# Gated delta rule: the triangular solve by 32x32 blocks inverted on VectorE, in place of 16x16 blocks joined on TensorE

## The reference, cut to what matters

```
# per head and chunk
Lmat = where(strict, (kb @ k.T) * decay, 0)         # strictly lower triangular
A    = Lmat + eye
rhs  = concat([v * beta, kb * exp(G)])
sol  = triangular_solve(A, rhs, lower, unit_diagonal)   # u, w
v_new = u - w @ S
o     = (q * exp(G)) @ S + attn @ v_new
S     = S * exp(G_last) + k_dec.T @ v_new
```

## Time and profile before

| | |
|---|---|
| median of 3 runs | 2217.33 us (2216.49 to 2218.11) |
| span of the profiled execution | 2215.9 us |
| mean granted TensorE clock | 0.995 |
| TensorE busy | 2178.7 us, 98% of the span |
| VectorE busy | 1499.2 us, 68% |
| ScalarE busy | 1004.1 us, 45% |

### The profile page before, as it was taken

One profiled execution on the slowest core, in us unless ns is written; L12 is line 12 of the kernel. 1 busy time (PEld: TensorE's weight loads), 2 busy tenths in 40 slices (PEclk: granted clock), 3 DMA queues, 4 the chain that ended last, 5 costly groups with the idle time before them and its releaser, 6 DMA issues.

```text
span 2215.9 us, 27209 instructions
## 1 busy us (share of the span) xinstructions
PE 2178.7 (98%) x10552; PEld 1830.3 (83%) x10552; DVE 1499.2 (68%) x1881; ACT 1004.1 (45%) x1286; POOL 25.4 (1%) x26
## 2 busy tenths in 40 slices
PE   6899999999999999999999999999999999999998
PEld 5789988888888888888888888888888888888887
DVE  8988698988888677755455555575546555655556
ACT  5357455433444644443444334465444444444444
POOL 0001000000000000000000000000000000000000
PEclk9999999999999999999999999999999999999999
DMA  9975568977998688866666666666666666666663
GB/s 404 420 275 166 186 220 279 305 244 245 331 337 302 207 277 292 295 219 191 192 191 186 191 197 190 187 203 192 190 197 185 191 194 191 189 192 189 194 190 128
DMA packets 241552, 507.08 MB, mean 229 GB/s; under 512 B 19304, under 2 KB 34960, under 8 KB 235920
## 3 DMA queue, kind: packets, MB, share of 16 engines
q1 hardware_dynamic: 241424, 505.35, 70.2%
HBM read 503.16 MB, written 2.12 MB: 228 GB/s over the span
## 4 chain that ended last, share of the span: by engine, by line
PE 86%; DVE 6%; DMA 4%; ACT 2%; issue 2%; POOL 0%; DVEq 0%; ACTq 0%; POOLq 0%
PE bank L1254 25%; PE bank L1256 25%; PE bank L1255 25%; DVE WL L2080 2%; PE bank L1445 2%; PE bank L1186 2%; PE bank L1261 1%; PE bank L1263 1%; PE bank L1262 1%; DVE RAW L2067 1%; ACT WH L1528 1%; DMA RAW<-in_w_cd_dram 1%; DMA RAW<-in_w_ada_dram 1%; DMA A<-in_w_cq_dram 1%; DMA RAW<-in_w_cq_dram 1%
## 5 line engine op out<-in xcount | busy, mean ns | idle before, releaser
L2080 DVE TENSOR_TENSOR WL<-RAW,WH 128x1024 fp32r<-128x1024 f32 x706 | 859.9, 1222 | 576.7 <-ACT WH L1528 567.3
L1528 ACT CAST WH<-RAW 128x1024 fp32r<-128x1024 f32 x706 | 738.4, 1049 | 849.1 <-PE bank L1256 702.0
L1254 PE MATMUL bank<-WH,HTh 128*128 128x512 f32 x1922 | 758.1, 394 | 1.1 <-DVE WL L2080 1.0
L1256 PE MATMUL bank<-WH,HTl 128*128 128x512 f32 x1922 | 749.1, 390 | 0.0
L1255 PE MATMUL bank<-WL,HTh 128*128 128x512 f32 x1922 | 748.4, 389 | 0.0
L1256 PEld LDWEIGHTS bank<-WH,HTl 128*128 128x128 f32 x1922 | 360.8, 188 | 76.2
L1254 PEld LDWEIGHTS bank<-WH,HTh 128*128 128x128 f32 x1922 | 361.1, 188 | 75.7 <-DVE WL L2080 2.4
L1255 PEld LDWEIGHTS bank<-WL,HTh 128*128 128x128 f32 x1922 | 361.2, 188 | 72.2
L1254 PE MATMUL bank<-WH,R2h 128*128 128x512 f32 x408 | 160.6, 394 | 0.3 <-DVE WL L2080 0.3
L1256 PE MATMUL bank<-WH,R2l 128*128 128x512 f32 x408 | 159.0, 390 | 0.0
L1255 PE MATMUL bank<-WL,R2h 128*128 128x512 f32 x408 | 158.9, 389 | 0.0
(11 more groups left out here) (302 smaller groups left out, 1823.5 us busy)
## 6 DMA issues: line engine op xcount, KB each, us to landing
RAW<-in_a_w_in_dram SPq DMA_DIRECT2D x192, 512.0 KB, 4.2
RAW<-in_w_gate_up_dram SPq DMA_DIRECT2D x176, 512.0 KB, 4.5
RAW<-in_w_ada_dram SPq DMA_DIRECT2D x128, 512.0 KB, 5.5
RAW<-in_w_in_dram SPq DMA_DIRECT2D x112, 512.0 KB, 4.8
RAW<-in_w_down_dram SPq DMA_DIRECT2D x88, 512.0 KB, 4.3
RAW<-in_a_w_out_dram SPq DMA_DIRECT2D x64, 512.0 KB, 4.1
A<-in_w_ada_dram SPq DMA_DIRECT2D x17, 1024.0 KB, 14.0
RAW<-in_w_o_dram SPq DMA_DIRECT2D x32, 512.0 KB, 5.9
```

The costliest lines, as they stand in the source:

```text
L1254: e.matmul(o, ah[:, s], hi[:, k, :], start=first, stop=False)
L1256: i = e.matmul(o, al[:, s], hi[:, k, :], start=False, stop=last)
L1528: e.copy(hi, rv).then_inc(S["hi"], 1)
L2080: e.tensor_tensor(lo, rv, hi.bitcast(F32), ALU.subtract).then_inc(S["lo"], 1)
```

## The change

The diagonal blocks that VectorE inverts are 32x32 now. The column steps run over j = 0 to 30; step j works on (31 - j) rows of min(j + 1, 16) elements per partition, each step again one multiply and one add. They are put in 13 slots (`INV_STEPS`) in place of eight. `X`, `ZT` and `XZ` are gone: a cell spreads one matrix (`XT`) and goes on with `NT`, two slots after it. The layout steps around the inversion change with the block size.

```
-        for j in range(0, 15, 2):
-            self.put("inv", j, j + 2)
+INV_STEPS = [(0, 3), (3, 6)] + [(j, j + 2) for j in range(6, 24, 2)] + [(24, 27), (27, 31)]
+        for j0, j1 in INV_STEPS:
+            self.put("inv", j0, j1)
             yield
...
-        for name in ("X", "ZT", "XZ", "NT") + ("kS",) * tt + ("U", "NU", "NW", "NY", "o"):
+        for name in ("X", "NT") + ("kS",) * tt + ("U", "NU", "NW", "NY", "o"):
...
             for q in range(4):                                   # gdn_pick, ScalarE
                 r = slice(32 * q, 32 * q + 32)
                 e.copy(L.LP[r, :, :, n:n + 4].rearrange("p j b h -> p h b j"),
-                       lm[r, :, r].rearrange("p h (b j) -> p h b j", j=16)).then_inc(S["gdn_pick"], 1)
+                       lm[r, :, r].unsqueeze(2).to_broadcast([32, 4, 2, 32])).then_inc(S["gdn_pick"], 1)
...
+            for b in range(2):                                   # inv_x, ScalarE, 512 elements each
+                e.activation(L.XE[:, :, b, :], L.XB, ACT.Copy, scale=L.bm2[:, b:b + 1]).then_inc(S["gdn_pick"], 1)
...
+            e.transpose(L.LT..., L.LP...)                        # inv_in: 1024 elements, was 512
+            for b in range(2):                                   # was: three operations of 256 elements
+                e.tensor_scalar(L.XB[:, 16 * b:16 * b + 16, :], L.CID, L.bm2[:, b:b + 1], None, ALU.mult).then_inc(S["inv"], 1)
...
+            for j in range(*args):                               # inv
+                n, w = 31 - j, min(j + 1, 16)
+                rows, t, shape = L.XB[:, j + 1:32, 0:w], L.XP.rearrange("p i c -> p (i c)")[:, 0:n * w], [P, n, w]
+                t = t.rearrange("p (i c) -> p i c", c=w)
+                W.wait_ge("inv", 2 * j + 3)
+                e.tensor_tensor(t, L.LT[:, j, j + 1:32].unsqueeze(2).to_broadcast(shape),
+                                L.XB[:, j:j + 1, 0:w].to_broadcast(shape), ALU.mult).then_inc(S["inv"], 1)
+                W.wait_ge("inv", 2 * j + 4)
+                e.tensor_tensor(rows, rows, t, ALU.add).then_inc(S["inv"], 1)
...
-            for n in range(2):                                   # inv_out: two transposes of 512
-                W.wait_ge("gdn_pick", 2 * n + 18)
-                e.transpose(L.XO[n].rearrange("p n (b j) -> p j b n", b=2), L.XE[n]
-                            ).then_inc(S["inv"], 1)
+            W.wait_ge("gdn_pick", 18)                            # one transpose of 1024, one add of 512
+            e.transpose(L.XF.rearrange("p i b n -> p (i b n)"), L.XE.rearrange("p i b c -> p (i b c)")).then_inc(S["inv"], 1)
+            W.wait_ge("inv", 66)
+            e.tensor_tensor(L.XO.rearrange("p n i -> p i n"), L.XF[:, :, 0, :], L.XF[:, :, 1, :], ALU.add).then_inc(S["inv"], 1)
...
-    elif name == "ZT":                                           # TensorE, one each per cell
-        W.wait_ge(dve, d("XT"))
-        each(a, Lm, XT).then_inc(mine, 1)
-    elif name == "XZ":
-        W.wait_ge(dve, d("ZT"))
-        each(b, X, q).then_inc(mine, 1)
     elif name == "NT":
-        W.wait_ge(dve, d("XT2"))
+        W.wait_ge(dve, d("XT"))
         each(a, Lm, XT).then_inc(mine, 1)
...
     if name == "X":                                              # VectorE
-        W.wait_ge("inv", 36)
+        W.wait_ge("inv", 67)
-        spread_blocks(X, L.XO[0])
-        spread_blocks(XT, L.XO[1])
+        spread_blocks(XT, L.XO)
-    elif name == "ZT":
-        e.tensor_tensor(q, a, bm4(L.pair), ALU.mult).then_inc(mine, 1)
-    elif name == "XZ":
-        e.tensor_tensor(XT, XT, b, ALU.add).then_inc(mine, 1)
```

More of the change, by code:

```diff
@@ L20 @@
 KB = 256
-C_ID, C_ONE, C_INV, C_NH, C_COL, C_POS, C_C, C_TRI, C_PAIR = 0, 128, 256, 288, 296, 552, 554, 576, 704
-C_OFF, C_CM, C_BM, C_ID16, C_AL, C_DT, C_GN, C_END = 832, 960, 1088, 1096, 1352, 1360, 1368, 1496
+C_ID, C_ONE, C_INV, C_NH, C_COL, C_POS, C_C, C_TRI = 0, 128, 256, 288, 296, 552, 554, 576
+C_OFF, C_CM, C_BM, C_ID16, C_AL, C_DT, C_GN, C_END = 704, 832, 960, 968, 1224, 1232, 1240, 1368
 CS = 3 * P + 80
@@ L36, in shape_constants @@
     c[:, C_TRI:C_TRI + P] = row <= col
-    c[:, C_PAIR:C_PAIR + P] = (row // 32 == col // 32) & (row % 32 < 16) & (col % 32 >= 16)
     c[:, C_OFF:C_OFF + P] = row // 32 < col // 32
@@ L189, in __init__ @@
         self.CID = C[:, C_ID16:C_ID16 + 256].rearrange("p (i j) -> p i j", j=16)
-        self.pair, self.off, self.bm2 = C[:, C_PAIR:C_PAIR + P], C[:, C_OFF:C_OFF + P], C[:, C_BM:C_BM + 2]
+        self.off, self.bm2 = C[:, C_OFF:C_OFF + P], C[:, C_BM:C_BM + 2]
         self.bm4 = C[:, C_BM + 2:C_BM + 6]
@@ L252, in __init__ @@
         self.SS = [ar(96, 512).rearrange("p (h d) -> p h d", d=P), ar(98, 512).rearrange("p (h d) -> p h d", d=P)]
[L253 to L258, removed]
+        self.LP = ar(40, 1024).rearrange("p (j b n) -> p j b n", b=2, n=16)
+        self.LT = ar(44, 1024).rearrange("p (j i) -> p j i", i=32)
+        self.XB, self.XP = (ar(kb, w).rearrange("p (i c) -> p i c", c=16) for kb, w in ((48, 512), (50, 256)))
+        self.XE = ar(52, 1024).rearrange("p (i b c) -> p i b c", b=2, c=16)
+        self.XF = ar(40, 1024).rearrange("p (i b n) -> p i b n", b=2, n=16)
+        self.XO = ar(12, 512).rearrange("p (n i) -> p n i", i=32)
         self.cell = [[ar(64 + 16 * g + 2 * i, 512).rearrange("p (h d) -> p h d", d=P) for i in range(8)] for g in range(2)]
@@ L903, in solve @@
             yield
-        for name in ("X", "ZT", "XZ", "NT") + ("kS",) * tt + ("U", "NU", "NW", "NY", "o"):
+        for name in ("X", "NT") + ("kS",) * tt + ("U", "NU", "NW", "NY", "o"):
             at(name)
             yield
-            if name in ("X", "ZT", "XZ", "NT"):
+            if name in ("X", "NT"):
                 yield
@@ L1075, in cell_values @@
     if tt == 0:
[L1076 to L1079, removed]
+        return (["NT", "U", "NU", "NW", "NY", "o", "S"],
+                ["XT", "kd", "R", "NT", "W", "V", "S", "ss", "n1", "n2"], ["U", "Y", "o", "sq"])
+    return (["NT", "kS", "qS", "U", "NU", "NW", "NY", "o"],
+            ["XT", "NT", "R1", "R2", "R3", "QS", "W", "V", "o", "ss", "n1", "n2"], ["U", "Y", "sq"])
 def count_cells():
@@ L1464, in pe_cell @@
         held[nb] = [(dve, d("at"))]
-    elif name == "ZT":
+    elif name == "NT":
         for n in (na, nb):
@@ L1469, in pe_cell @@
         W.wait_ge(dve, d("XT"))
-        each(a, Lm, XT).then_inc(mine, 1)
-    elif name == "XZ":
-        W.wait_ge(dve, d("ZT"))
-        each(b, X, q).then_inc(mine, 1)
-    elif name == "NT":
-        W.wait_ge(dve, d("XT2"))
         each(a, Lm, XT).then_inc(mine, 1)
@@ L1715, in act_program @@
                 e.copy(L.LP[r, :, :, n:n + 4].rearrange("p j b h -> p h b j"),
-                       lm[r, :, r].rearrange("p h (b j) -> p h b j", j=16)).then_inc(S["gdn_pick"], 1)
+                       lm[r, :, r].unsqueeze(2).to_broadcast([32, 4, 2, 32])).then_inc(S["gdn_pick"], 1)
         elif kind == "inv_x":
-            W.wait_ge("inv", 34)
-            for n in range(2):
-                src = L.XB if n else L.XB.rearrange("p i j -> p j i")
-                for b in range(2):
-                    e.activation(L.XE[n][:, :, b, :], src, ACT.Copy, scale=L.bm2[:, b:b + 1]).then_inc(S["gdn_pick"], 1)
+            W.wait_ge("inv", 65)
+            for b in range(2):
+                e.activation(L.XE[:, :, b, :], L.XB, ACT.Copy, scale=L.bm2[:, b:b + 1]).then_inc(S["gdn_pick"], 1)
         elif kind == "z":
@@ L2292, in dve_program @@
             W.wait_ge("cst_in", 32)
[L2293 to L2299, removed]
-                                   ).then_inc(S["inv"], 1)
-        elif kind == "inv":
[L2303 to L2306, removed]
+            e.transpose(L.LT.rearrange("p j i -> p (j i)"), L.LP.rearrange("p j b n -> p (j b n)")).then_inc(S["inv"], 1)
@@ L2307, in dve_program @@
                 W.wait_ge("inv", 2 * j + 4)
-                e.tensor_tensor(t, L.LB[:, j + 1:16, j:j + 1].to_broadcast(shape),
-                                L.XB[:, j:j + 1, 0:j + 1].to_broadcast(shape), ALU.mult).then_inc(S["inv"], 1)
-                W.wait_ge("inv", 2 * j + 5)
                 e.tensor_tensor(rows, rows, t, ALU.add).then_inc(S["inv"], 1)
         elif kind == "inv_out":
-            for n in range(2):
-                W.wait_ge("gdn_pick", 2 * n + 18)
-                e.transpose(L.XO[n].rearrange("p n (b j) -> p j b n", b=2), L.XE[n]
-                            ).then_inc(S["inv"], 1)
+            W.wait_ge("gdn_pick", 18)
@@ L2607, in dve_cell @@
     elif name == "X":
-        W.wait_ge("inv", 36)
+        W.wait_ge("inv", 67)
         W.wait_ge(own, CELL["dve", 1, "atm"] if tt == 0 else CELL["dve", 0, "n2"])
-        spread_blocks(X, L.XO[0])
-        spread_blocks(XT, L.XO[1])
+        spread_blocks(XT, L.XO)
         if tt == 0:
             e.tensor_tensor(k, k, bc4(L.eD[:, 0, hs]), ALU.mult).then_inc(mine, 1)
-    elif name == "ZT":
-        W.wait_ge(pe, m("ZT"))
```

(5 more changed lines are left out.)

## The result

The changed kernel takes 2221.0 us (median of 19 runs, 2219.9 to 2222.7), the kernel before 2217.3 us (19 runs, 2215.8 to 2218.5) on the same chip. The ratio is 1.0018, with a 95% interval from 1.0012 to 1.0024: slower by 3.7 us, somewhere between 2.7 and 5.3. The forecast was +4.6 us, 2221.9. The profiled executions have spans of 2219.1 and 2215.9 us, 3.2 apart. The page tells almost nothing of where this lies. These are the lines that answer to the earlier trace rows.

What follows compares the result with a forecast made beforehand. TensorE, busy 98% of the span, was taken as the bound. Waits of 13.5 us less 1.7 before and 7.2 of products gave +4.6: span 2215.9 to 2220.5, median 1.4 above, 2221.9 us; range 2219.2 to 2225.6.

Steps and rivals of the forecast that it cites:

- Eight groups of products at 0.90 us: TensorE in the four cells: two groups of four float32 products gone per cell, 7.2 us saved, all counted.
- the four waits after half 121: TensorE's waits for the spread (NT, twice), NW's add and X or NU, about 0.5 us each, 1.9 us together.
- The inversion's 20.7 us on VectorE: 62 operations at 0.195 us + 1.04 ns per element, 20.7 us for 6.5 before, so 14.2 us more.
- The first rival: Inversion steps j = 2 to 26: pace stays at 0.26 us per operation, giving -1.3 us, 2216.0; chance 0.07.
- other estimate, 19.6 us: The inversion on VectorE by the Trainium skill's fixed term of about 150 cycles at 0.96 GHz for each of 62 operations.
- The layout steps at nothing: VectorE's inv_in and inv_out around the inversion were to stay at about 1.9 us each, adding nothing.
- the slow transpose of the upper bound: In inv_in and inv_out, a transpose of 1024 elements could cost 2.1 us for 1.24, +1.8 us for both.
- The split of half 121: VectorE needs 55.4 us from 400.15 to its end at 455.5; half 121 starts at 455.7, 11.6 us late.
- The place: From about 411 to 456 us TensorE waits for VectorE's splits about ten times, 10 to 12 us together.
- waits under 8 us: Sign of a wrong prediction: TensorE's waits for splits sum to under 8 us, meaning a pace per operation below the line.
- The other sign: Sign of a wrong prediction: the time moves after 560 us, where nothing was expected.
- The waits, 13.5 after and 1.7 before: TensorE's waits for VectorE: 11.6 us up to half 121 and 1.9 behind it, against 1.7 in the kernel before.

Runs made afterwards that it cites:

- seven: The kernel before (16x16 blocks, both joining products) with five's units table and its 15 column steps in 15 slots in place of 8: 2217.5 us, ratio 1.0003.
- five: The changed kernel with its 31 steps in 23 slots and the w_ada units around the inversion moved to where VectorE has room: 2209.2 us against 2217.4.
- Six: The kernel before with ZT and XZ cut from four heads to one on TensorE, VectorE's work and all waits kept: 2213.8 us, ratio 0.9984.
- one: The changed kernel with two groups of four products put back per cell ahead of NT, their results overwritten: 2225.7 us against 2217.1 for the kernel before.
- two: The changed kernel with each of the 62 inversion operations cut to one column, the inverse left unfinished: 2212.1 us, ratio 0.9978 to the kernel before.
- three: The changed kernel with the same 31 steps in 23 slots in place of 13: 2216.0 us, ratio 0.9992 to the kernel before.
- four: The changed kernel with eight w_ada units moved from the inversion's slots to z and the first two gb jobs: 2214.7 us, ratio 0.9988 to the kernel before.

## Why the prediction was right, point by point

- *Eight groups of products at 0.90 us, all counted.* Right as a sum, and shown where nothing waits: 7.4 us between the traces of seven and five. Six and one show the limit: next to a VectorE without a lead part of a product only fills a wait. Six gave back 2.7 us of 5.4 by the traces (3.6 by the medians), one cost 6.1 of 7.2. The forecast had this in its walk (the four waits after half 121), not in its sentence "I count all of it".
- *The inversion's 20.7 us on VectorE.* Summed over the 13 slots (first multiply to the start of what follows, 399.78 to 401.21, ..., 444.02 to 445.80), the trace has 20.4 us. One line through the rows of 15, 64 and 512 elements held for all sizes between. The first rival (a pace that stays flat) was wrong by the same rows, and two shows that the elements carry their 8.7 us. The prediction's other estimate, 19.6 us, is 0.8 too low.
- *The layout steps at nothing.* `inv_in` took 398.64 - 397.00 = 1.64 us for 1.93, since both small operations together took 0.48; `inv_out` took 452.71 - 450.49 = 2.22 for 1.95, since its add with a permuted output runs 1.11 us for 512 elements, where the cells' operations of 512 run 0.68. Together nothing, but by two errors that cancel: neither term was right for its reason, and that is luck. Both transposes of 1024 elements took 1.24 us, so the slow transpose of the upper bound did not come. A pick on ScalarE takes 0.67 us now, for 0.43 before; no wait came of it.
- *The split of half 121.* 55.4 us of VectorE from the start of the inversion; the trace has 399.78 to 455.03, 55.25 us. Half 121 starts at 455.16, for 455.7.
- *The place.* About ten waits from 411 to 456 us were forecast, 10 to 12 us together. The profile lists seven of 7.9 us. It lists idle time only; half 121 starts 50.16 us after half 107 (405.00), and 14 halves alone take 38.1, so the loss is 12.1 us: idle time, slower restarts, and one half at a lower clock. By the words of the forecast ("waits under 8 us") the list speaks against it, by 0.1 us, and the reason given there (a pace below the line) is not the cause, as the pace was on the line: the bound should have been put on the distance, not on the list. The other sign, a change after 560 us, is absent: from the first half of `og` to the end it is 1597.7 us before and 1597.3 after.
- *The size, +4.6 for +3.7.* The interval (2.7 to 5.3) holds both. The forecast gave 0.55 to more than 4.4 us and 0.42 to a change within it, and the measured 3.7 lies within. The traces say which terms made up the difference. They also differ in entry: half 107 starts at 406.00 before and at 405.00 after, VectorE's first transpose at 397.09 and 397.00. From half 107 to the first half of `og` the changed kernel takes 4.6 us more (212.2 and 216.8), but 3.6 if counted by the span's clock (618.16 and 621.79), as VectorE, which sets the pace, began at the same time. The 4.6 that equals the forecast is therefore chance. TensorE's head start of 1.0 us was not the change's: the trace of six, whose code is that of before up to there, has half 107 at 404.96. A head start of TensorE is worth nothing in a stretch that VectorE paces.
- *The waits, 13.5 after and 1.7 before.* Five, nearly free of waits, is the measure: its 203.6 us from half 107 to `og`. The changed kernel takes 13.2 more, 12.2 without the head start, so the forecast is 1.3 too high. Of this 0.5 lie ahead of half 121 (it starts 58.2 us after VectorE's first transpose, for 58.6 forecast), and 0.8 behind it, where the forecast had 1.9 us of waits and experiment one puts them at about 1.1. The kernel before takes 8.6 more than five, of which 7.2 to 7.4 are products, so its own loss is 1.2 to 1.4 us for 1.7. Together (1.3 less 0.3 to 0.5) that is the 1.0 us, nearly, by which the forecast lies above the traces' 3.6.

## What to carry to other kernels

Before work is moved from the bound engine to another, follow the other engine's lead through that very stretch: here it was 68% busy over the kernel and 98% where the work was to go, and 7 us of saved products were outweighed by 12 us of lost time. Spare time of an engine lies in certain slots; the same work put there (or other work of that engine moved from where it is short) gave 8 us instead of costing 4. A walk along both engines' orders, slot by slot, with durations from one trace missed the changed kernel and experiments three, five, six and seven by 0.9, 0.5, 0.2, 0.0 and 1.5 us, which is within what these measurements can tell (their intervals are 2.6 to 5.5 us wide) but for the last; counting each product or unit at its whole time missed one by 2.4 us and four by 1.6 to 3.3.

## What the runs showed of the hardware

From 120 to 2200 us the granted clock fell in only one of the nine traces, the changed kernel's, and there once. These are windows of the changed kernel, and then of experiment one, around the longest wait (2.13 and 2.14 us) for a split; the last three columns are granted clock, DMA share and GB/s.

```profile
415.00:431.00 16.00, 11.87 (x48) 8.70 (x48) 15.59 (x29) 5.18 (x5) 0.00 (x0) 1.00 0.75 242
431.00:435.00 4.00, 3.47 (x9) 2.72 (x10) 3.90 (x8) 1.05 (x1) 0.00 (x0) 0.59 0.77 243
```

```profile
414.00:430.00 16.00, 11.88 (x48) 8.70 (x48) 15.59 (x29) 5.15 (x5) 0.00 (x0) 1.00 0.74 239
430.00:434.00 4.00, 3.02 (x12) 2.18 (x12) 3.90 (x8) 1.04 (x1) 0.00 (x0) 1.00 0.82 256
```

In the changed kernel TensorE ran at the lower level, 1.2 GHz, for most of 431 to 435 us (0.59 on average): matmuls 0.43 us apart for 0.23. In experiment one the same work after the same wait stayed at 2.4 GHz. What decides between them is not shown. These are the starts of half 115, the next one, in the changed kernel and in experiment one.

```profile
435.98 0.40 PE L1254 MATMUL bank<-WH,HTh 128*128 128x512 f32 x1
```

```profile
434.25 0.50 PE L1254 MATMUL bank<-WH,HTh 128*128 128x512 f32 x1 [0.80 <-DVE WL L2074]
```

Experiment one stands 1.1 us earlier by VectorE's clock, so without the drop half 115 would have started at 435.35: the drop cost 0.6 us there. At full clock TensorE waited 0.80 us for the split at this place; at the lower one it had no need to, since the split was ready at 435.22. By half 118 nothing of the 0.6 us is left (444.22 and 443.13, again 1.1 apart), since VectorE sets the pace. The drop made no difference to the time.
